# Moving the copy of a finished attention tile to the start of the next step of the loop, on VectorE alone

## The reference, cut to what matters

```python
def mixer(p, kv, lw, rope):                      # first block, for the tokens and (layer 0) the context
    f_in, c_q, q_g, gate_logits = ...            # parts of one projection
    y_f = fourier_mix(f_in) @ lw["w_fo"]         # real part of a 2D FFT over tokens and 128 features, 4 groups
    ...
    y_m = attend(q_m, k_m, v_m) @ lw["w_mo"]     # 8 heads
    y_g = attend(q_g, k_g, v_g) @ lw["w_go"]     # 8 heads on 2 key/value heads
    return (g_f * y_f + g_m * y_m + g_g * y_g) @ lw["w_o"]

# inside attend, per block of 128 queries
s = einsum("bqkgd,btkd->bkgqt", q, k); w = softmax(s); o = einsum("bkgqt,btkd->bqkgd", w, v)
```

## Time and profile before

| | |
|---|---|
| median of 3 executions | 2835.73 us (2834.24 to 2836.42) |
| the profiled execution | 2834.24 us |
| its span in the profile | 2832.3 us |
| share of the span busy | PE 97%, PEld 86%, DVE 33%, ACT 44%, POOL 62% |
| chain that ended last | PE 87%, DVE 5%, ACT 3%, DMA 2%, POOL 1% |
| granted TensorE clock over the span | 0.989 |
| first attention (layer 0) | about 165 to 385 us, L2918 from 185.4 us |
| second attention (layer 1) | about 1048 to 1173 us, last L2918 at 1172.3 us |

### The profile page before, as it was taken

The page is one execution under the profiler, slowest core; times in us unless marked ns, Lnnn a source line. Parts: engine busy times, 40 slices in busy tenths (PEclk is TensorE's granted clock), DMA queues, the critical chain, the costliest instruction groups (busy, mean ns, idle before and its releaser), DMA issues.

```text
span 2832.3 us, 48340 instructions
## 1 busy us (share of the span) xinstructions
PE 2744.6 (97%) x19897; PEld 2433.1 (86%) x19897; DVE 947.6 (33%) x1905; ACT 1247.8 (44%) x1667; POOL 1756.2 (62%) x1336
## 2 busy tenths in 40 slices
PE   7999999999999899999999999999999999999999
PEld 5766678768888677898989999999999999989999
DVE  3144431341211534443233223454312314354330
ACT  4335532342322446544444444555434435554443
POOL 1402054434454242687978978558998987757996
PEclk8999999999999999999999999999999999999999
DMA  7554623222323244554545567435555557534553
GB/s 222 138 166 148 209 86 93 90 71 93 102 92 97 54 146 151 165 164 150 195 148 176 181 159 215 124 116 169 188 181 166 187 178 187 166 105 156 179 182 122
DMA packets 401894, 418.93 MB, mean 148 GB/s; under 512 B 78891, under 2 KB 371875, under 8 KB 401424
## 3 DMA queue, kind: packets, MB, share of 16 engines
q1 hardware_dynamic: 401712, 416.37, 47.5%
HBM read 415.27 MB, written 3.16 MB: 148 GB/s over the span
## 4 chain that ended last, share of the span: by engine, by line
PE 87%; DVE 5%; ACT 3%; DMA 2%; POOL 1%; issue 1%; SPq 1%; DVEq 0%; ACTq 0%; POOLq 0%
PE ps L931 31%; PE ps L915 23%; PE ps L899 16%; PE ps L942 15%; PE ps L959 2%; POOL ring_r L1819 1%; DMA ring<-in_w_in 1%; ACT ring_hi L1872 1%; DMA ring<-in_w_ada 1%; ACT arena L2120 1%; DVE arena L2951 1%; DVE stat L2937 1%; DVE hT_r L3186 0%; SPq L583 0%; DMA ring<-in_w_branch_gla 0%
## 5 line engine op out<-in xcount | busy, mean ns | idle before, releaser
L1819 POOL TENSOR_TENSOR ring_r<-ring,ring_hi 128x512 fp32r<-128x512 f32 x1328 | 1754.0, 1355 | 1047.2 <-ACT ring_hi L1872 1019.1
L931 PE MATMUL ps<-hT_r,ring_hi 128*128 128x256 f32 (+1 forms) x5952 | 863.1, 303 | 7.4 <-POOL ring_r L1819 3.3
L931 PEld LDWEIGHTS ps<-hT_r,ring_hi 128*128 128x128 f32 x5952 | 796.0, 190 | 62.3 <-issue 14.9
L1872 ACT ACTIVATE ring_hi<-ring 128x2048 fp32r<-128x2048 f32 x312 | 596.4, 1912 | 428.3 <-DMA ring<-in_ffn_w_down 151.4
L915 PE MATMUL ps<-arena_r,ring_hi 128*128 128x256 f32 (+1 forms) x2784 | 438.8, 303 | 7.1 <-DVE arena L3224 3.1
L942 PE MATMUL ps<-hT_r,ring_r 128*128 128x256 f32 (+1 forms) x2976 | 441.2, 301 | 0.0
L942 PEld LDWEIGHTS ps<-hT_r,ring_r 128*128 128x128 f32 x2976 | 402.1, 190 | 19.6
L915 PEld LDWEIGHTS ps<-arena_r,ring_hi 128*128 128x128 f32 x2784 | 385.7, 190 | 30.4 <-DVE arena L3224 3.9
L915 PE MATMUL ps<-arena_r,ring_r 128*128 128x256 f32 (+1 forms) x1392 | 242.3, 302 | 0.0
L915 PEld LDWEIGHTS ps<-arena_r,ring_r 128*128 128x128 f32 x1392 | 201.6, 190 | 10.3
L899 PE MATMUL ps<-arena 128*64 128x128 f32 (+9 forms) x1616 | 184.4, 339 | 9.4 <-ACT arena L2106 3.3
(11 more groups left out here) (344 smaller groups left out, 2687.8 us busy)
## 6 DMA issues: line engine op xcount, KB each, us to landing
ring<-in_w_in SPq DMA_DIRECT2D x74, 1024.0 KB
ring<-in_w SPq DMA_DIRECT2D x64, 1024.0 KB
ring<-in_w_ada SPq DMA_DIRECT2D x48, 1024.0 KB
ring<-in_ffn_w_up SPq DMA_DIRECT2D x44, 1024.0 KB
ring<-in_ffn_w_gate SPq DMA_DIRECT2D x44, 1024.0 KB
ring<-in_ffn_w_down SPq DMA_DIRECT2D x44, 1024.0 KB
ring<-in_w_in SPq DMA_DIRECT2D x48, 256.0 KB
ring<-in_w_o SPq DMA_DIRECT2D x8, 1024.0 KB
```

The costliest lines, as they stand in the source:

```text
L931: mm = pe.matmul(o, w[0], a[x], start=j == 0 and x == 0, stop=False, skip_group_check=True)
L1819: ins = pool.tensor_tensor(k.ring_lo[s][:, part], k.ring[s][:, part], k.ring_hi[s][:, part], ALU.subtract)
L1872: act.activation(k.ring_hi[s][:, :], k.ring[s][:, :], ACT.Copy).then_inc(k.hi_ready[s], 1)
```

## The change

The two lines that call `moved` go from the place behind `modulations()` in odd steps to a place ahead of `probabilities(u - 1)` in the even step that follows. The tiles that are moved are the same; the call `moved(len(todo) - 1)` behind the loop stays.

```diff
                 for u in range(len(todo) + LAG):
                     if LAG <= u:
                         skip(2)
+                    if u >= 4 and u % 2 == 0:
+                        moved(u - 3)
                     if 1 <= u <= len(todo):
                         probabilities(u - 1)
                     if u < len(todo):
@@
                     modulations()
                     if u == 0:
                         skip(1)
-                    if 3 <= u < len(todo) + 1 and u % 2:
-                        moved(u - 2)
                     if second:
                         half, g = second
                         even_odd(g, HALVES[half][0], *T.take())
```

## The result

| | before | after |
|---|---|---|
| median of 4 executions each | 2835.82 us (2834.24 to 2836.42) | 2854.70 us (2852.97 to 2857.37) |
| ratio after / before | | 1.0068 [1.0051, 1.0086] |
| the profiled execution | 2834.24 us, span 2832.3 | 2854.13 us, span 2852.3 |
| granted TensorE clock over the span | 0.989 | 0.985 |

The change makes the kernel slower by 0.68%, 19 us of the median, with an interval of 14 to 24 us. The forecast was 2846.7 us with a range up to 2850.5: the sign was right, the size too small.

The account below looks back on a forecast made before the run. TensorE, busy 97% of the span, was taken to bound the kernel and to wait for the copy L2918; 8.55 us in layer 0 plus 2.5 in layer 1 gave 11.0, so 2835.7 + 11.0 = 2846.7 us, range 2840.5 to 2850.5.

Parts of the forecast that it names:

- Step 3 of both layers: Only the three DFT copies go ahead of the copy and fit VectorE's idle time: 0.1 us slower in each layer.
- Steps 5, 7 and 9 of layer 0: First attention: copy behind `even_odd` and three DFT copies, so TensorE goes on 1.6, 1.6 and 2.5 us later.
- Steps 17 and 19: Layer 0: copy behind L2991; TensorE 1.15 us later, then 1.6 us, taken from 1.8 because of waits for `w_ada`.
- Step 11 of layer 0 and step 9 of layer 1: Cost 0 each: `even_odd` fits VectorE's idle time in the first; the wait for GpSimd hides about 0.8 us in the second.
- Layer 1, steps 5, 7 and 11: Second attention: 2.05 us slower at step 5, 0.4 us gained at step 7, 0.75 us slower at step 11.
- The credit for step 7: Layer 1: `even_odd` goes into the wait for TensorE, so the reciprocal starts 0.52 us earlier; 0.4 us gained.
- The sum of the stalls: All moved places of both attentions: 8.55 us in layer 0 and 2.5 in layer 1, together 11.0 us slower.
- No change: Rival: the bank was free early enough or later TensorE waits give the time back; sum 4.4 us; chance 0.1.
- faster: Rival: VectorE no longer blocked in front of the PV tile, TensorE's next waits shrink; at best -6 us, 2829.7; chance 0.04.
- The third rival: Stalls make VectorE late too, adding up where it has no idleness; 15 to 18 us slower, 2852; chance 0.06.
- What would show it: Profile after: TensorE's waits for L2918 up 10 to 12 us, busy times unchanged, shift some 8.5 us from 390 us.
- The other page's rule on rotating banks: Perfetto Trace Analysis, Matmuls: groups rotating through PSUM banks overlap evacuation with the next group's matmuls; copy hidden anywhere, sum 0.

Follow-up runs that it names:

- The constant products: Changed kernel plus products of constants into the transposes' bank ahead of the transposes of steps 6, 8, 10, 18 and 20 of layer 0: 2844.22 us.
- half of the way: Kernel before, but in steps 5, 7 and 9 of layer 0 the copy stands behind `even_odd` and ahead of the three DFT copies: 2843.26 us.
- the late copy with the scores first: Changed kernel with the scores ahead of the transposes on TensorE in even steps from 4 on: 2842.65 us.
- the late copy with the early product: Changed kernel with the product with the values ahead of DFT and dense products in steps 3 to 11 (odd) of layer 0 and 3, 5, 7, 11 of layer 1: 2860.71 us.

## Why the prediction was right in sign and wrong in size

- *What bounds the kernel* was right. TensorE waits for the copy, at the places named, and every microsecond of stall counted above reached the end of its attention.
- *Step 3 of both layers*, 0.1 us each: 0.13 more in layer 0 (0.82 for 0.69), 0.07 less in layer 1 (0.62 for 0.69). Right as near as it matters, and the run with only the DFT copies ahead shows why: they fit into the idle time.
- *Steps 5, 7 and 9 of layer 0*, 1.6, 1.6 and 2.5 us of stall: measured 1.57, 1.57 and 2.47. Right to 0.03 us each. The copy comes in the row L2925, L2928, L2979, L2981, L2982 as foreseen, but VectorE did idle ahead of the row, 1.51 us for L2138, since `even_odd` now meets that wait itself; the forecast had used that wait for the start and only described the row's end.
- *Steps 17 and 19*, 1.15 and 1.6 us: 1.16 and 1.89. The forecast took 0.2 off for the waits for `w_ada`, with 0.5 as the most; they disappeared, and 0.7 was given back.
- *Step 11 of layer 0 and step 9 of layer 1*, 0: the stall of step 12 is 0.69 us in both traces. In layer 1 the stall of step 10 is 0.76, and the wait for GpSimd hides it, 0.48 instead of 1.31. Both right, the second with its reason.
- *Layer 1, steps 5, 7 and 11*, 2.05 - 0.4 + 0.75: measured 2.1, 0 and 0.8. The credit for step 7 was not paid: the shift is 18.31 at 1083.6 us and 18.30 at 1106.8 and 1117.4 us (times of before). The reciprocal did start 0.52 us earlier against the copy. But the two L2951 behind it ran beside a GpSimd instruction and took 2.08 us instead of 1.77, and the maxima behind those start when TensorE's scores are there, 2.7 us after the copy's start in both traces. (In the trace of before, the 79 L2951 with no GpSimd instruction beside them take at most 490 ns, the 17 with one 819 to 1531.)
- *The sum of the stalls*, forecast 11.0: measured 8.8 + 2.9 = 11.7 us, and 11.0 with the 0.7 given back at `w_ada`. That it is the same to a tenth is luck in part, since 0.4 of credit too much in layer 1 and 0.5 too little at step 20 about cancel.
- *The step that failed* is the one from the stalls to the time: "VectorE and ScalarE wait for those scores, so the whole pipeline moves and no engine can make it good". It let the time grow by the stalls' sum and nothing else, as if TensorE went on behind a stall as fast as before. The missing term is the lower clock behind the stalls of steps 6, 8, 10 and 20 of layer 0: 1.6 + 3.1 + 1.5 + 1.4 = 7.6 us in this trace. The constant products took it away together with the drop of the clock, while the lateness of everything else stayed. The 20 us of the two spans are then 11.0 + 7.6 and the 1.4 outside the attentions. The trace of the kernel before had the sign: it holds stretches of half clock too, one at 578 us, where TensorE waits 0.70 and 1.08 us for VectorE and then 3.19 (columns as above):

```profile
570.00:578.00 8.00, 6.12 (x30) 3.48 (x29) 3.48 (x25) 2.05 (x5) 0.00 (x0) 1.00 0.00 0
578.00:589.00 11.00, 7.60 (x17) 4.97 (x17) 5.90 (x9) 5.22 (x10) 0.00 (x0) 0.53 0.30 95
```

- *Rivals.* "No change" and "faster" are out. The third rival, 2852 us, came near the measured time with a mechanism that the traces do not show: it had VectorE late without idleness from step to step, 0.3 us at each of 12 places and 0.8 in steps 9 and 11. Step 12 of layer 0 is unchanged, and layer 1 grew by its stalls only, the one of step 10 hidden. A number that fits proves no mechanism; the run that keeps TensorE busy was needed to tell them apart.
- *What would show it.* The waits for the copy rose from 3.2 to 11.6 us between 165 and 345 us, and in the whole span by 12.3 us, a little above the "10 to 12 us" given (0.8 of it is the hidden stall). The shift by 390 us was foreseen as 8.5, and was 18.0 - 2.3 = 15.7. The busy time of PE was to stay the same, and grew by 8.0 us: of all rows of the page this one says at a glance that the stalls are not all. Of the 20 us, 2.3 at the start, -1.8 between the attentions and 0.9 behind them lie where no instruction moved, and executions of one kernel differ by as much.

One sentence of the Trainium skill bears on this. TensorE: Matmul & The Clock Gate tells in its section What's actually happening that the engine has two clock levels, and that work ahead of a stretch decides which is granted; the rows after (0.53 and 0.66 behind stalls, 1.00 with the constant products) agree, though not every stall of the same length was followed by the lower level; had the forecast weighed it, the range would have reached further up. The other page's rule on rotating banks, by which the prediction got a sum of 0, did not hold for this round: after the change the transposes wait for L2918 twelve times.

## What to carry to other kernels

A copy that frees a PSUM bank belongs where the next user of that bank, found by walking the round, will not wait; work can go ahead of it for nothing as long as it waits for nothing itself and fits the idle time. On an engine that bounds a kernel, price a new stall at its length plus what the matmuls behind it lose if the clock drops, take the second from rows of the trace at the lower level, and look at busy time and granted clock after. If a stall can't be removed, bring independent work into it or keep TensorE multiplying something, and measure: that one run here gained by it is no rule, as the kernel before already has such products ahead of the waits at 575 us, and its clock falls there all the same.

## What was not expected of the hardware

- Where the copy came late, single waits of TensorE of 1.48 to 2.47 us, between stretches in which it was busy, were followed by some microseconds at half the granted clock: behind 1.73, 1.73, 2.47 and 2.12 in the changed kernel, 1.72, 1.72 and 2.46 with only steps 5, 7 and 9 late, 2.11 with only 17 and 19, 1.74 with half of the way, 1.48 in the late copy with the scores first, and 1.87, 2.11 and 2.17 (layer 1) in the late copy with the early product. Behind single waits for the copy of up to 1.41 us it never was; but two waits close together, 0.70 and 1.08 us at 575 us of the kernel before, were.
- It does not follow from the length alone: behind 2.03 us in layer 1 (changed kernel, only layer 1 late, constant products) and behind stalls of 1.54, 1.87 and 2.61 (the late copy with the early product) the clock stayed. The wait of 1.7 us for L2918 near the end of layer 1's attention, which 12 of the 13 traces have, that of the kernel before too, was followed by half clock in one. At the end of layer 0's attention 11 of the 13 traces have a wait of 1.87 or 1.88 us for ScalarE with the same instructions around it, and half clock follows in 3 of them, at a cost of some 1.4 us. Only steps 17 and 19 late, and before:

```profile
364.48 1.97 PE L900 MATMUL ps<-arena 128*64 128x128 f32 x16 [1.88 <-ACT arena L2107]
```

```profile
360.14 1.09 PE L899 MATMUL ps<-arena 128*64 128x128 f32 x16 [1.88 <-ACT arena L2106]
```

  What decides is open; I didn't find it in these runs.
- Executions of one kernel differ by up to 8 us (33 of the kernel before, 2834.2 to 2842.2), and traces of programs that are the same up to there differ by up to 5.6 us by 165 us, with different clocks in the first 60 us (0.86 and 0.89 in the two profiles compared here). A change of a few microseconds can't be read off two spans without the shift at a place ahead of it.
